# Attention: p times v in two passes over v's two parts, sums of p on VectorE, remainders of p on GpSimd

## The chip, the cores and the metric

One core of a Trainium2 chip runs the whole program in one launch. The metric is the device time of that launch in microseconds, the median of several runs. Five engines work side by side, each through a list of instructions of its own: TensorE (PE, with its weight loads as PEld), VectorE (DVE), ScalarE (ACT), GpSimd (POOL) and SyncE (SP), which here issues most of the transfers. They meet through semaphores alone.

## The reference, cut to what matters

Two requests, of 1024 (prompt) and 2048 (sample) tokens, pass through one layer: RMSNorm, a projection, two groups of attention heads side by side (8 GQA heads over 2 key heads of width 64, and 8 MLA heads of width 96), an output projection, a mixture of experts and a last norm. Both requests see 16 learned meta tokens ahead of their own keys. For each head and each request:

```python
s = jnp.einsum('bqhgd,bkhd->bhgqk', q, k, preferred_element_type=jnp.float32) * scale
p = jax.nn.softmax(s, axis=-1).astype(v.dtype)
return jnp.einsum('bhgqk,bkhe->bqhge', p, v)
```

Everything is float32. The change touches how `p` times `v` and the sums of `p` are computed.

## The kernel before, in words

The program has six stages after each other. The first, `stage_project`, makes q, k and v for all heads and stores them; the second, `stage_attend`, is attention; the four behind it are not touched.

TensorE multiplies in fp32r, which keeps fewer bits than float32. To keep the accuracy, a float32 matrix is written as a high part (rounded to fp32r) and a low part (the remainder, rounded too), and products are added up in several passes.

**Steps of a head.** `ITEMS` lists the work of a head. The queries are taken 512 at a time (six blocks: four of the sample request, two of the prompt). Within a block an item is one group of 128 keys, and one item at the end holds the 16 meta keys; so a sample block has 17 items, a prompt block 9, a head 86. "Step j" is what each engine does around item j:

- TensorE, `qk` (L1071): scores of 128 keys by 512 queries into one of two banks `psS`, two passes in a GQA head, three in an MLA head.
- ScalarE, `exp` (L940, L943): the exponential twice, once rounded as `p_hi`, once in full as `prob`. A meta item has a third one (L942).
- VectorE, `remainder` (L988): `p_lo = prob - p_hi`. Every eighth item from 24 on is done by GpSimd instead (L929), 8 a head. Slots for p are four.
- TensorE, `pv` (L1094), two steps behind: three passes into `psO` with v's part as weights, 64 columns and a column of ones, whose product is the denominator: v_hi with p_hi, v_lo with p_hi, v_hi with p_lo.

**Maxima for the next head.** The exponentials need a maximum for each query beforehand. So during head h, TensorE also makes a rough score of head h+1 (L1102, one pass, 128 queries by 512 keys, bank `psM`, two of them), and VectorE takes its maximum (L996). These are the 80 `UNITS`, spread over 72 of the 86 steps. The meta keys have 24 small products of 16 columns of their own (L1108), all at one step. At step 79 the maxima are turned (`row`, L1115), written to DRAM and read back as one row of q of head h+1 (L863, L866); TensorE waits for it before the next head's first scores.

**End of a block.** ScalarE copies `psO` out (L949), TensorE turns it in four pieces of 65 (L1121), VectorE takes the reciprocal of the denominator and multiplies (`normalise`, L1019, L1022), and the result is stored.

**Loads.** SyncE loads q, k, v of head h+2 in two parts: the sample part once item 67 of head h is through `pv`, then comes the row store of head h+1, then the prompt part at the end of the head. GpSimd splits the loaded v into v_hi and v_lo (`split`, L905, L916).

**The order** is written out by hand: each engine's function walks the same items, and numbers such as `j - 2` for `pv` or `j - 6` for `normalise` say how far behind it works. The heads lie in two loops of two heads a turn, with the last pairs of each kind written out.

In `stage_project` the copy of GQA's v is GpSimd's (L334), MLA's v comes out of a bank `psX` by ScalarE (L416); the two banks of `psX` serve "v", "k", "n", "r", "s" units in turn, and TensorE waits for the bank to be free (L651 for the "k" units).

## Time and profile before

| what | us |
|---|---|
| median of 3 runs | 4235.22 (4228.05 to 4240.24) |
| profiled execution | 4237.25 |
| its span, first to last instruction | 4235.1 |
| TensorE busy in the span | 3738.5 |
| VectorE busy | 2819.2 |
| ScalarE busy | 2366.1 |
| GpSimd busy | 429.1 |
| stage_project, about | 0 to 560 |
| stage_attend, about | 560 to 2875 |

The span counts from the first to the last instruction of the profiled execution; the time of that execution is 2.15 us longer. Busy time is the union of the listed durations on one engine. On TensorE a listed duration includes the way through the array, so that consecutive matmuls overlap in the list. "Released by" names what a waiting instruction waited for, as inferred from semaphores. A duration "x2" in the order in time is the merged length of two instructions in a row.

### The profile page before, as it was taken

Reading aid. Unit: us, or ns where it says so; the run is one execution under the profiler, and the core shown is the slowest. Engines: PE = TensorE matmul, PEld = TensorE weight load, DVE = VectorE, ACT = ScalarE, POOL = GpSimd, SP = SyncE. Lnnn points to the kernel's source line nnn. Section 1 sums busy time; section 2 is a strip of 40 time slices with the busy share of each in tenths; the row PEclk is TensorE's granted clock in tenths of the full one; section 3 lists DMA queues with packets and bytes.
Section 4 is the critical chain, followed back from the end, with each engine's and each line's share of the span. In section 5 each row is a group of like instructions: output and inputs, shape, how many; then the busy total and the mean of one; then the engine's idle time right before and its main releaser. Section 6 shows DMA issues by size and latency. Waiting matters only on the chain. (4 is left out here: it accounts for less than half of the span.)

```text
span 4235.1 us, 60176 instructions
## 1 busy us (share of the span) xinstructions
PE 3738.5 (88%) x16747; PEld 2738.7 (65%) x16748; DVE 2819.2 (67%) x4468; ACT 2366.1 (56%) x4059; POOL 429.1 (10%) x497
## 2 busy tenths in 40 slices
PE   7999856999999999999999999996999499999920
PEld 7989724666666666666666766765777366666610
DVE  5656545888878888777776877743443666666645
ACT  4434303777777777776676766784332155555522
POOL 0000010111111111111011011000000011110123
PEclk9999957999999999999999999998999699999965
DMA  4555574221222211221122022003333277777768
GB/s 161 167 194 194 166 166 160 60 46 26 54 60 60 59 40 28 60 59 42 24 59 60 16 48 60 6 7 141 137 125 113 84 254 249 248 248 248 248 211 295
DMA packets 330198, 495.54 MB, mean 117 GB/s; under 512 B 118791, under 2 KB 261411, under 8 KB 318915
## 3 DMA queue, kind: packets, MB, share of 16 engines
q1 hardware_dynamic: 241798, 359.85, 28.8%
q10 hardware_dynamic: 71888, 73.54, 5.0%
q0 software_dynamic: 16272, 59.25, 4.1%
q8 instruction: 115, 1.88, 0.2%
q14 instruction: 125, 1.02, 0.1%
HBM read 330.84 MB, written 161.78 MB: 116 GB/s over the span
## 5 line engine op out<-in xcount | busy, mean ns | idle before, releaser
L940 ACT ACTIVATE b_p_hi<-b_psS 128x512 fp32r<-128x512 f32 (+1 forms) x1376 | 822.1, 597 | 620.2 <-PE b_psS L1071 579.5
L1071 PE MATMUL b_psS<-b_q,b_k 96*128 96x512 f32 (+3 forms) x3440 | 1053.2, 404 | 53.5 <-ACT b_prob L943 31.6
L988 DVE TENSOR_TENSOR b_p_lo<-b_prob,b_p_hi 128x512 fp32r<-128x512 f32 x1152 | 830.1, 722 | 287.5 <-ACT b_prob L943 248.5
L943 ACT ACTIVATE b_prob<-b_psS 128x512 f32<-128x512 f32 (+1 forms) x1376 | 815.1, 592 | 1.1
L1071 PEld LDWEIGHTS b_psS<-b_q,b_k 96*128 96x128 f32 (+3 forms) x3440 | 629.8, 186 | 285.0 <-ACT b_prob L943 39.2
L996 DVE TENSOR_REDUCE b_mx_s<-b_psM 128x1 f32<-128x512 f32 x1024 | 690.8, 687 | 86.8 <-PE b_psM L1102 66.1
L1102 PE MATMUL b_psM<-b_k,b_q 128*128 128x512 f32 (+1 forms) x1280 | 515.8, 424 | 54.5 <-DMA b_v<-V 39.2
L1094 PE MATMUL b_psO<-b_p_hi,b_v_hi 128*65 128x512 f32 x1280 | 516.9, 404 | 25.8 <-DVE b_p_lo L988 23.9
L1094 PE MATMUL b_psO<-b_p_hi,b_v_lo 128*65 128x512 f32 x1280 | 509.7, 398 | 0.0
L1094 PE MATMUL b_psO<-b_p_lo,b_v_hi 128*65 128x512 f32 x1280 | 509.6, 398 | 0.0
L1102 PEld LDWEIGHTS b_psM<-b_k,b_q 128*128 128x128 f32 (+1 forms) x1280 | 251.8, 197 | 158.2 <-DVE b_mx_s L996 53.1
L929 POOL TENSOR_TENSOR b_p_lo<-b_prob,b_p_hi 128x512 fp32r<-128x512 f32 x128 | 166.7, 1302 | 1720.0 <-ACT b_prob L943 1720.0
L1094 PEld LDWEIGHTS b_psO<-b_p_lo,b_v_hi 128*65 128x65 f32 x1280 | 175.8, 137 | 125.5 <-issue 5.7
L1094 PEld LDWEIGHTS b_psO<-b_p_hi,b_v_hi 128*65 128x65 f32 x1280 | 176.7, 138 | 118.8 <-DVE b_p_lo L988 52.1
L1094 PEld LDWEIGHTS b_psO<-b_p_hi,b_v_lo 128*65 128x65 f32 x1280 | 177.6, 139 | 110.1 <-issue 4.3
L2016 PE MATMUL e_psG<-e_w_gu,e_xT 128*128 x512 | 232.1, 596 | 9.0 <-SPq L1863 8.0
L612 PE MATMUL a_psZ<-a_w_hi,a_xT_hi 128*128 128x396 f32 x600 | 209.2, 349 | 24.2 <-DVE a_w_lo L569 24.2
L1965 DVE TENSOR_TENSOR e_wd_lo<-e_w_dn,e_wd_hi 128x2048 fp32r<-128x2048 f32 x64 | 146.7, 2293 | 104.0 <-ACT e_wd_hi L1914 104.0
L612 PE MATMUL a_psZ<-a_w_hi,a_xT_lo 128*128 128x396 f32 x600 | 206.9, 345 | 0.0
L612 PE MATMUL a_psZ<-a_w_lo,a_xT_hi 128*128 128x396 f32 x600 | 206.3, 344 | 0.0
L996 DVE TENSOR_REDUCE b_mx_p<-b_psM 128x1 f32<-128x512 f32 x256 | 173.9, 687 | 30.8 <-PE b_psM L1102 27.6
L1900 ACT ACTIVATE e_wg_hi<-e_w_gu 128x2048 fp32r x64 | 122.9, 1920 | 98.1 <-SPq L1863 74.7
(246 smaller groups left out, 5184.9 us busy)
## 6 DMA issues: line engine op xcount, KB each, us to landing
e_w_gu<-w_gate SPq DMA_DIRECT2D x32, 1024.0 KB
e_w_gu<-w_up SPq DMA_DIRECT2D x32, 1024.0 KB
e_w_dn<-w_down SPq DMA_DIRECT2D x32, 1024.0 KB
Y<-e_y ACTq DMA_DIRECT2D x64, 512.0 KB, 5.3
Y<-b_zeros ACTq DMA_DIRECT2D x4, 4096.0 KB, 27.3
a_x_raw<-xallT SPq DMA_DIRECT2D x25, 512.0 KB, 5.0
a_x<-xall SPq DMA_DIRECT2D x25, 512.0 KB, 4.4
c_o<-O SPq DMA_DIRECT2D x24, 512.0 KB, 4.9
```

Source lines behind the costliest of these rows:

```text
L612: i = nc.tensor.matmul(psZ[:, b, 0:ZW], xx[:, s, c, :], ww[:, c, b * ZW:b * ZW + ZW], start=n == 0, stop=n == 3 * KC - 1)
L929: nc.gpsimd.tensor_tensor(p_lo[:, slot, :], prob[0:kn, slot, :], p_hi[0:kn, slot, :].bitcast(F32), ALU.subtract).then_inc(lo_ready_pool, 1)
L940: nc.scalar.activation(p_hi[0:kn, (s * NI + j) % NP, :], psS[0:kn, j % 2, :], ACT.Exp)
L943: nc.scalar.activation(prob[0:kn, (s * NI + j) % NP, :], psS[0:kn, j % 2, :], ACT.Exp).then_inc(p_ready, 1)
L988: nc.vector.tensor_tensor(out, prob[0:kn, slot, :], p_hi[0:kn, slot, :].bitcast(F32), ALU.subtract).then_inc(lo_ready, 1)
L996: nc.vector.tensor_reduce(dst, psM[:, u % 2, :], AX.X, ALU.max).then_inc(m_free, 1)
L1071: m = nc.tensor.matmul(psS[0:kn, j % 2, :], kk[s][0:r, k], qq[s][0:r, q], start=n == 0, stop=n == len(passes) - 1)
L1094: m = nc.tensor.matmul(psO[0:VC, b % 2, :], vv[s][:, vc, :], pp[:, slot, :], start=first and n == 0, stop=last and n == 2)
L1102: nc.tensor.matmul(psM[:, u % 2, :], q0[s][0:r, q * P:q * P + P], k0[s][0:r, kc:kc + 512], start=True, stop=True).then_inc(m_psum, 1)
L1900: nc.scalar.activation(wg_hi[:, :, :], w_gu[:, bass.ds(w * KC, HK), :], ACT.Copy).then_inc(wg_rounded, 1)
L1965: nc.vector.tensor_tensor(wd_lo[:, c, :], w_dn[:, bass.ds(w * HC, HC), :], wd_hi[:, c, :].bitcast(F32), ALU.subtract).then_inc(wd_ready, 1)
L2016: nc.tensor.matmul(psG[:, s, :], xT[:, c - HK, :], w_gu[:, bass.ds(w * KC + c, 1), :].rearrange("p o n -> p (o n)"), start=c == HK, stop=F ...
```

## The change

- v is kept as its two parts side by side: 128 columns, high and low, made once in `stage_project` (GpSimd subtracts for GQA, VectorE for MLA) and loaded as such. The column of ones goes. `pv` has two passes, v with p_hi (`pv_hi`, two steps behind) and v with p_lo (`pv_lo`, four steps behind); rows 0 to 63 of the result belong to v's high part and 64 to 127 to its low part, and are added in `normalise`. So p_lo times v's low part is now in the sum as well.
- The denominators: VectorE adds every `prob` of a block into a PSUM bank `acc` (`den_add`), the last sum goes to `accS`; TensorE turns it, VectorE sums along the keys.
- All remainders of 128-key items go to GpSimd; a meta item's stays on VectorE. p has six slots, not four, and a slot is free when both `pv_lo` and the sum are done.
- The meta item is second in a block. The meta keys are stored beside the prompt's and beside the sample's keys, so the maxima see them too: 104 units of 346 to 414 keys over 68 steps, and the 24 small products go. The loads get 3 or 4 more transfers of 16 columns per part.
- `row` is at step 77, the turn of the results at 6 steps behind a block's end (was 5) and with eight transposes of 128x128, `normalise` at 7 (was 6).

```diff
-VC = VD + 1
+VC = 2 * VD
...
+        BY_ACT, BY_DVE = "vkn", "vknrs"
...
+                src = z[:, s, ZV:ZCQ].rearrange("p (h c) -> p h c", c=VD)
                 for copy in range(2):
-                    i = nc.gpsimd.tensor_copy(vst_g[:, b, j, copy:PAIRS:2, 0:VD],
-                                              z[:, s, ZV:ZCQ].rearrange("p (h c) -> p h c", c=VD))
+                    nc.gpsimd.tensor_copy(vst_g[:, b, j, copy:PAIRS:2, 0:VD].bitcast(F32R), src)
+                pool.drain()
+                for copy in range(2):
+                    i = nc.gpsimd.tensor_tensor(vst_g[:, b, j, copy:PAIRS:2, VD:VC].bitcast(F32R), src,
+                                                vst_g[:, b, j, copy:PAIRS:2, 0:VD], ALU.subtract)
                 i.then_inc(v_copied, 1)
...
+                    if kind == "v":
+                        r = META if B is None else P
+                        i = nc.vector.tensor_tensor(vst_m[0:r, j, :, VD:VC].bitcast(F32R),
+                                                    psX[0:r, u % 2, :].rearrange("p (h c) -> p h c", c=VD),
+                                                    vst_m[0:r, j, :, 0:VD], ALU.subtract)
+                    elif kind == "k":
...
+        CUT_S, CUT_P = [414, 414, 412, 412, 412], [348, 346, 346]
+        assert sum(CUT_S) == META + DEC_SEQ and sum(CUT_P) == META + SEQ
...
-        for base, n in ((SEQ, DEC_SEQ), (0, SEQ)):
+        for base, n, k_at, meta_at in ((SEQ, DEC_SEQ, SAMPLE, META_S), (0, SEQ, 0, META_P)):
             for qc in range(base, base + n, W):
-                ch = [(META + base + c * P, P, (base + c * P) // P) for c in range(n // P)] + [(0, META, TILES)]
+                ch = [(k_at + c * P, P, (base + c * P) // P) for c in range(n // P)]
+                ch.insert(1, (meta_at, META, TILES))
...
+        UNITS = []
+        for first, tiles, at, cuts in ((SEQ // P, DEC_SEQ // P, META_S, CUT_S), (0, SEQ // P, 0, CUT_P)):
+            for i in range(tiles):
+                UNITS += [(first + i, at + sum(cuts[:u]), cuts[u], u) for u in range(len(cuts))]
         NU = len(UNITS)
-        R = 4
-        SPAN = 72
+        R = 6
+        HI_LAG, LO_LAG = 2, 4
+        SPAN = 68
...
+                    q, k, sm = slice(SEQ, TOK), (slice(META_S, SAMPLE), slice(SAMPLE, KT)), ld_s[s]
+                    kd = (slice(0, META), slice(META + SEQ, KEYS))
...
+                    for c, d in zip(k, kd):
+                        dma(k0[s][0:GD, c], t["KGH"][rk, d])
+                        dma(k0[s][GD:P, c], t["KGH"][rk, d])
+                        dma(k1[s][0:GD + 1, c], t["KGL"].rearrange("g r n -> (g r) n")[bass.ds(i * (GD + 1), GD + 1), d])
...
+            def remainder(h, s, j):
+
+                if ITEMS[j][2] == META:
+                    return
+                slot = slot_of(s, j)
+                pool.wait_ge(p_ready, h * NI + j + 3)
+                nc.gpsimd.tensor_tensor(p_lo[:, slot, :], prob[:, slot, :], p_hi[:, slot, :].bitcast(F32),
+                                        ALU.subtract).then_inc(lo_ready, 1)
...
+                act.wait_ge(pv_done, h * NI + j + 1 + NP - reuse(s, j))
+                act.wait_ge(den_done, h * NI + j + 1 + NP - reuse(s, j))
+                slot = slot_of(s, j)
+                nc.scalar.activation(p_hi[0:kn, slot, :], psS[0:kn, j % 2, :], ACT.Exp)
+                nc.scalar.activation(prob[0:kn, slot, :], psS[0:kn, j % 2, :], ACT.Exp).then_inc(p_ready, 1)
...
+            def den_add(h, s, j):
+
+                _, _, kn, _, first, last = ITEMS[j]
+                slot = slot_of(s, j)
                 dve.wait_ge(p_ready, h * NI + j + 3)
-                out = p_hi[M_HI2, slot, :] if kn == META else p_lo[:, slot, :]
-                nc.vector.tensor_tensor(out, prob[0:kn, slot, :], p_hi[0:kn, slot, :].bitcast(F32),
-                                        ALU.subtract).then_inc(lo_ready, 1)
+                if kn == META:
+                    nc.vector.tensor_tensor(p_hi[M_LO, slot, :], prob[0:kn, slot, :], p_hi[0:kn, slot, :].bitcast(F32),
+                                            ALU.subtract).then_inc(meta_lo_ready, 1)
+                dve.wait_ge(den_done, h * NI + j + NP)
+                if first:
+                    m = nc.vector.tensor_copy(acc[:, :], prob[:, slot, :])
+                else:
+                    out = accS[:, BLOCK_OF[j] % 2, :] if last else acc[0:kn, :]
+                    m = nc.vector.tensor_tensor(out, acc[0:kn, :], prob[0:kn, slot, :], ALU.add)
+                m.then_inc(den_done, 1)
...
-                tv = psT[:, 0:SUP * VC].rearrange("p (j c) -> p j c", c=VC)
-                nc.vector.reciprocal(rden[:, :].unsqueeze(2), tv[:, :, VD:VC])
+                tv = psO[:, b % 2, :].rearrange("p (j c) -> p j c", c=P)
+                nc.vector.tensor_reduce(den[:, :], psT[:, :].rearrange("p (j c) -> p j c", c=P), AX.X, ALU.add)
                 dve.drain()
+                nc.vector.reciprocal(rden[:, :], den[:, :])
+                dve.drain().then_inc(t_free, 1)
                 dve.wait_ge(o_stored[b % 2], 16 * (h * (NB // 2) + b // 2 + 1))
-                nc.vector.tensor_tensor(ost[:, b % 2, :, :], tv[:, :, 0:VD],
-                                        rden[:, :].unsqueeze(2).broadcast_to([P, SUP, VD]), ALU.mult).then_inc(o_ready, 1)
-                dve.drain().then_inc(t_free, 1)
+                rr = rden[:, :].unsqueeze(2).broadcast_to([P, SUP, VD])
+                nc.vector.tensor_tensor(o_lo[:, :, :], tv[:, :, VD:2 * VD], rr, ALU.mult)
+                nc.vector.tensor_tensor(ost[:, b % 2, :, :], tv[:, :, 0:VD], rr, ALU.mult)
+                dve.drain()
+                nc.vector.tensor_tensor(ost[:, b % 2, :, :], ost[:, b % 2, :, :], o_lo[:, :, :], ALU.add).then_inc(o_ready, 1)
...
+            def pv_hi(h, s, j):
+                _, _, kn, vc, first, _ = ITEMS[j]
+                b = BLOCK_OF[j]
+                if kn == META:
+                    return
+                pe.wait_ge(p_ready, h * NI + j + 3)
                 if first:
...
+                    cc = slice(c * P, c * P + P)
+                    nc.tensor.transpose(psO[:, b % 2, cc], oT[:, b % 2, cc], ident[:, :])
+                    m = nc.tensor.transpose(psT[:, cc], accS[:, b % 2, cc], ident[:, :])
...
-                    pv(h, s, j - 2, block_of[j - 2])
-                    if j - 5 in END_OF:
-                        o_turn(h, END_OF[j - 5], use(h, END_OF[j - 5], last))
+                    pv_hi(h, s, j - HI_LAG)
+                    pv_lo(h, s, j - LO_LAG)
+                    if j - 6 in END_OF:
+                        o_turn(h, END_OF[j - 6], use(h, END_OF[j - 6], last))
...```

Two places in the order of instructions, with what each waits for. VectorE, GQA heads, where a block's normalise stands between two steps; `b_psM` is the bank of maxima, `b_psT` the bank the results are turned into. Before:

```order
L988 TENSOR_TENSOR b_p_lo<-b_prob,b_p_hi 128x512 [waits b_p_ready]
L994 REGISTER_ALU
L996 TENSOR_REDUCE b_mx_s<-b_psM 128x1 [waits b_m_psum]
L1017 REGISTER_ALU
L1019 RECIPROCAL b_rden<-b_psT 128x4 [waits b_t_psum]
L1022 TENSOR_TENSOR b_ost<-b_psT,b_rden 128x256 [waits b_o_stored1]
L986 REGISTER_ALU
L988 TENSOR_TENSOR b_p_lo<-b_prob,b_p_hi 128x512 [waits b_p_ready]
```

After the change:

```order
L1000 TENSOR_TENSOR b_acc<-b_acc,b_prob 128x512 [waits b_den_done]
L1006 REGISTER_ALU
L1008 TENSOR_REDUCE b_mx_s<-b_psM 128x1 [waits b_m_psum]
L1006 REGISTER_ALU
L1008 TENSOR_REDUCE b_mx_s<-b_psM 128x1 [waits b_m_psum]
L1025 REGISTER_ALU
L1027 TENSOR_REDUCE b_den<-b_psT 128x4 [waits b_t_psum]
L1029 RECIPROCAL b_rden<-b_den 128x4
L1033 TENSOR_TENSOR b_o_lo<-b_psO,b_rden 128x256 [waits b_o_stored1]
L1034 TENSOR_TENSOR b_ost<-b_psO,b_rden 128x256
L1036 TENSOR_TENSOR b_ost<-b_ost,b_o_lo 128x256
L995 REGISTER_ALU [waits b_p_ready]
```

A sum takes the place of each remainder, some steps have two maxima, and normalise has five instructions for two. TensorE, GQA heads, around one step. Before:

```order
L1071 MATMUL b_psS<-b_q_0,b_k_0 128x512 [waits b_p_ready]
L1071 MATMUL b_psS<-b_q_0,b_k_0 128x512
L1102 MATMUL b_psM<-b_k_1,b_q_1 128x512 [waits b_m_free] x2
L1094 MATMUL b_psO<-b_p_hi,b_v_hi 65x512 [waits b_lo_ready_pool]
L1094 MATMUL b_psO<-b_p_hi,b_v_lo 65x512
L1094 MATMUL b_psO<-b_p_lo,b_v_hi 65x512
```

After the change:

```order
L1115 MATMUL b_psM<-b_k_1,b_q_1 128x412 [waits b_m_free] x2
L1096 MATMUL b_psO<-b_p_hi,b_v 128x512 [waits b_p_ready]
L1108 MATMUL b_psO<-b_p_lo,b_v 128x512 [waits b_lo_ready]
L1084 MATMUL b_psS<-b_q_0,b_k_0 128x512 [waits b_p_ready]
L1084 MATMUL b_psS<-b_q_0,b_k_0 128x512
```

The third pass is gone, the products with v are 128 wide, and the two of a step are of different items with a wait of their own.

## Rows read from the trace of the kernel before

**Rows 1.** Windows: us, then PE, PEld, DVE, ACT, POOL busy (x), clock, DMA, GB/s.

```profile
1300.00:1700.00 400.00, 392.51 (x1744) 265.71 (x1742) 344.47 (x561) 314.16 (x588) 55.91 (x47) 1.00 0.23 50
```

**Rows 2.** The order in time, one GQA step: start us, us, engine, line, operation.

```profile
1007.39 0.64 PE L1071 MATMUL b_psS<-b_q,b_k 128*128 128x512 f32 x2
...
1008.79 0.62 PE L1071 MATMUL b_psS<-b_q,b_k 128*128 128x512 f32 x2
...
1007.71 0.68 DVE L996 TENSOR_REDUCE b_mx_s<-b_psM 128x1 f32<-128x512 f32 x1
...
1008.31 0.68 DVE L988 TENSOR_TENSOR b_p_lo<-b_prob,b_p_hi 128x512 fp32r<-128x512 f32 x1
```

**Rows 3.** The order in time: meta-key products; then row stores; last, the stores' own line.

```profile
1421.27 0.39 PE L1090 MATMUL b_psO<-b_p_hi,b_v_meta 128*65 128x512 f32 x1
...
1445.49 0.39 PE L1090 MATMUL b_psO<-b_p_hi,b_v_meta 128*65 128x512 f32 x1
...
2400.32 0.40 PE L1090 MATMUL b_psO<-b_p_hi,b_v_meta 128*65 128x512 f32 x1
...
2428.27 0.40 PE L1090 MATMUL b_psO<-b_p_hi,b_v_meta 128*65 128x512 f32 x1
...
811.49 0.31 SPq L863 DMA_DIRECT2D MX<-b_nmxT  x1
...
1714.34 0.30 SPq L863 DMA_DIRECT2D MX<-b_nmxT  x1
...
L863 SPq DMA_DIRECT2D MX<-b_nmxT x16: 302/308/1948, 655.8 to 2737.4; - x16
```

**Rows 4.** The order in time, first stage: nine transposes of 128x128.

```profile
410.93 1.14 PE L623 MATMUL a_psR<-a_ident,a_stage 128*128 128x128 f32 x9
```

**Rows 5.** The order in time, VectorE: one block's normalise and what follows.

```profile
942.59 0.18 DVE L1019 RECIPROCAL b_rden<-b_psT 128x4 f32<-128x4 f32 x1 [0.17 <-issue]
...
942.93 0.42 DVE L1022 TENSOR_TENSOR b_ost<-b_psT,b_rden 128x256 f32<-128x256 f32 x1 [0.16 <-issue]
...
943.56 0.69 DVE L988 TENSOR_TENSOR b_p_lo<-b_prob,b_p_hi 128x512 fp32r<-128x512 f32 x1 [0.21 <-issue]
```

**Rows 6.** The page's part 5: remainders on GpSimd; busy, mean ns, idle before.

```profile
L929 POOL TENSOR_TENSOR b_p_lo<-b_prob,b_p_hi 128x512 fp32r<-128x512 f32 x128 | 166.7, 1302 | 1720.0 <-ACT b_prob L943 1720.0
```

**Rows 7.** The order in time beside GpSimd's split; then line 1022's min/median/max ns.

```profile
943.75 2.78 POOL L916 TENSOR_TENSOR b_v_lo<-b_v,b_v_hi 128x1040 fp32r<-128x1040 f32 x1
...
944.44 2.65 DVE L988 TENSOR_TENSOR b_p_lo<-b_prob,b_p_hi 128x512 fp32r<-128x512 f32 x1 [0.18 <-ACT b_prob L943]
...
L1022 DVE TENSOR_TENSOR b_ost<-b_psT,b_rden x96: 423/425/426, 727.9 to 2869.7; 128x256 f32<-128x256 f32 x96
```

**Rows 8.** The order in time, TensorE after three waits; then windows from 1080.

```profile
947.14 0.44 PE L1094 MATMUL b_psO<-b_p_hi,b_v_hi 128*65 128x512 f32 x1 [1.46 <-DVE b_p_lo L988]
...
1080.28 0.69 PE L1094 MATMUL b_psO<-b_p_hi,b_v_hi 128*65 128x512 f32 x1 [2.08 <-DVE b_p_lo L988]
1080.76 0.63 PE L1094 MATMUL b_psO<-b_p_hi,b_v_lo 128*65 128x512 f32 x1
...
957.77 1.22 PE L1071 MATMUL b_psS<-b_q,b_k 128*128 128x512 f32 x2 [4.95 <-issue]
...
1080.00:1085.00 5.00, 4.72 (x14) 2.69 (x15) 1.90 (x4) 2.27 (x5) 0.00 (x0) 0.66 0.05 12
```

**Rows 9.** The order in time, SyncE's issues; then one window while they run.

```profile
1320.03 0.49 SPq L828 DMA_DIRECT2D b_q<-QGH  x1
...
1336.03 1.95 SPq L863 DMA_DIRECT2D MX<-b_nmxT  x1
1340.40 0.23 SPq L866 DMA_DIRECT2D b_q<-MX  x1
...
1325.00:1335.00 10.00, 10.00 (x58) 7.26 (x56) 6.71 (x14) 6.96 (x14) 0.56 (x1) 1.00 1.01 215
```

**Rows 10.** Groups by line, first stage: the product that waits for v's eviction.

```profile
L651 PEld LDWEIGHTS a_psX<-a_ckvT,a_w_kup 128*128 128x128 f32 x104 | 18.8, 194 | 28.5 <-ACT a_vst_m L416 25.2 <-issue 1.3
```

243 lines of the change are left out of this document (95 added, 148 removed).

## The prediction

> **What bounds the kernel now.** I read the page first, then stretches of the attention stage, then single instructions there. The page puts TensorE first and VectorE second over the whole span. Attention alone is tighter: in 400 us of it TensorE is busy 392.5, VectorE 344.5, ScalarE 314.2 and GpSimd 55.9, at full clock [rows 1]. TensorE sets the pace there, with VectorE 14% behind.
>
> Busy time counts the whole length of an instruction, though the next one starts earlier, so I price by start to start. A 512-column matmul is listed as 0.39 us, but the next starts after 0.23: the six of a GQA step run from 1007.39 to 1008.79, so 0.232 each (1.40 a step), with 65 or with 128 columns of weights. On VectorE, remainder and maximum alternate at exactly 0.60, though listed as 0.68 [rows 2]. These two prices carry most of the sum.
>
> The spacing of one meta-key product to the next gives the time of a block. A sample block of 17 steps takes 24.2 us in a GQA head, 28.0 in an MLA head. The last head has no maxima to make; its blocks come to 23.2 by the prices (100 matmuls). The row of maxima is written once a head: 7 GQA heads take 1714.34-811.49, 129.0 each, and 7 MLA heads 2737.4-1714.34, 146.2 each [rows 3]. A check of the prices: a GQA head now has 498 full-width matmuls, 115.5 us, plus some 9 of narrow ones, transposes and stalls, against 126 to 134 measured.
>
> **The change on TensorE.** The third pass goes: 80 matmuls x 0.232 = 18.6 us a head. The 24 meta maxima of 16 columns go as well. Units become 104 instead of 80; at 412 columns one should take 0.19 us (0.232 less 100 columns at 2.4 GHz), so +1 us. The 24 narrow transposes become 48 of 128x128; nine such took 1.14 us [rows 4], so 6 us a head. A GQA sample block then needs 67x0.232 + 26x0.19 + 1.0 = 21.5 us, an MLA block 17 passes more, 25.4.
>
> **The change on VectorE.** The length of an instruction grows by 1.02 ns an element (128x256 is 0.42, 128x512 is 0.68 [rows 2, 5]), so a 412-column maximum costs 0.60-0.10 = 0.50. Per sample block:
> - 16 sums at 0.60 = 9.6. They replace 14 remainders; GpSimd had two.
> - The meta item has two dependent instructions, 2x0.69, and one of them reads two SBUF tensors and can wait for GpSimd, 0.5 on average: 1.9.
> - 26 maxima at 0.50 (now 19 at 0.60) = 12.9.
> - Normalise. Now: drain, reciprocal, drain, multiply, 1.14 us from the end of the work before to the next start [rows 5]. It gets a 512-element sum (0.69), a second multiply (0.34), an add (0.43) and two more gaps of 0.16, and the add can wait 0.5 for GpSimd: 3.3.
>
> Together 27.7 us, **more than TensorE needs in either kind of head**; by the same prices it is 22.2 now. For a whole head: 3 such blocks, plus 35 steps with two short blocks (32 sums 19.2, 3 meta items 5.7, 3 normalises 9.9, 26 maxima 12.3, row work 1.5 = 48.6): 131.7 us.
>
> No row shows a sum that reads and writes PSUM. From above it is bounded by the isolated 0.69, from below by 0.53 (512 elements at that slope); I take 0.60, since the maximum, which reads PSUM, and the remainder, which reads SBUF, keep the same pace in the same stretch [rows 2]. The ends are -6 and +8 us a head. The Trainium skill (VectorE: DVE Perf Modes, the section on the TRN2 errata) charges a PSUM source 120 cycles where an SBUF source pays 58. By that the estimate would be 65 ns more for each sum, some 5.5 us a head and about 85 us on the kernel. By that rule a maximum out of PSUM would last longer than a remainder out of SBUF; the trace has both at 0.68.
>
> **GpSimd** takes all 80 remainders of a head at 1.30 (1.32 with a gap) [rows 6], 104 us, and loses the splitting of v. Of the 27.7 of a block it needs 20.8, so VectorE covers it. Where the units end (18 steps) it needs about 21 against VectorE's 22. Only in the last head does it set the pace: 16 at 1.32 and 0.5 for the meta item, 21.6 a block against 23.2; with the short blocks 8 us in all.
>
> **Contention.** GpSimd's split already holds VectorE up: at 944.44 a remainder lasts 2.65 us beside a subtraction of 2.78 on GpSimd, while the multiply of PSUM with SBUF never varied, 423 to 426 ns over 96 [rows 7]. So I charge the port only where VectorE reads two SBUF tensors, and to the sums nothing. The Trainium skill (SBUF — State Buffer, "Who interferes with whom") states just this, that a second SBUF input contends and a single one does not; were the sums held all the same, see rival 2.
>
> **What lies between the sums.** VectorE will not be busy without a gap. Normalise comes in one lump of 3.3 us and TensorE can run only two maxima ahead, so it stalls some 2 to 3 us a block. After a stall of 1.46 it went on at full pace; after one of 2.08 its matmuls came 0.48 apart, and the slow spell of 3.5 us after it costs 1.7; the granted clock of that stretch, 0.66, mixes the 1.2 and the 2.4 GHz level [rows 8]. In a GQA head VectorE's backlog hides most of that; I charge 0.5 a block, 28.2. In an MLA head TensorE has 25.4 to do, and stall 2.0 plus clock 1.4 give 28.8.
>
> The row of maxima gets tight. The sample loads of the head after next (3.7 MB at 215 GB/s, 17 us and a start) begin at 1320.03 and so drain about 1338; the row store issued at 1336.03 lets its reload start only at 1340.40 [rows 9]. v's two halves make it 4.2 MB, 19.5 us, and the loads start two steps later (remainder pass four steps behind). That is 15 steps before the boundary, some 20 us, while drain, store and reload need 24. The other end is that v's 260-byte pieces, doubled, cost nothing: then 1.5 us are missing. I charge 2 us of idle VectorE a head, and 2 for the pause of 4.95 us at a loop's turn, which stays [rows 8]; 2 more in MLA heads. That makes GQA 3x28.2+48.6+3.8 = **137**, MLA 3x28.8+48.6+6 = **141**.
>
> **The first stage.** TensorE already waits for the eviction of v (25.2 us in total before the next product, over 12 batches) [rows 10]. Two subtractions of 0.69 now follow it before the bank is free: +0.75 a batch, 9 us. Its GpSimd subtractions lie behind matmuls. Larger first loads and more units before the first head: +3. Later stages are untouched.
>
> **Sum.** 8 GQA heads x (+8) = +64; 7 MLA heads x (-5.2) = -36; last head -8; +9; +3: +32. The profiled execution was 4237.25 around a span of 4235.1, 2 above the median of 4235.22, so against the median 4267.
>
> **Rivals.**
> 1. *The lumps are absorbed.* If VectorE really never waits (six slots of p instead of four let it lag), heads cost 131.7 of either kind: +2.7x8 -14.5x7 -8+12 = -76, so 4159, faster. For: all other engines then have slack. Against: maxima have two banks only, and waits for them occur already. It decides if the stall at normalise stays under 1.5 us. Chance 0.27.
> 2. *GpSimd's port holds the sums too.* Then 80 pairs cost 1.30+0.60 in turn, 152 a head before the other work: some +20 a head, 4560. [rows 7] speak against it. 0.05.
> 3. *Sums or stalls cost more.* Each sum takes the isolated 0.69 (+8 a head), or each lump ends at the 1.2 GHz level and the row waits 4 to 5 us (+4 to +7): 4330 to 4390. The page on VectorE's modes (the Trainium skill, above) gives much the same for the sums. 0.16.
> 4. *No gain from the narrower array use*: a 128-column v load could slow a pass; [rows 2] show 128-column passes at the same pace. With 0.03 more for each of 166 passes MLA heads would cost 5 more, 4300. 0.02.
>
> My own account, ending +0.3 to +2%, gets 0.34. Between it and rival 1 lies a balance within 0.3% (12.7 us, about what a measurement of this kernel can tell from no change), 0.14, and a small gain, 0.02. Slower: 0.34+0.05+0.16+0.02 = 0.57; faster: 0.27+0.02 = 0.29; same 0.14. The low end is rival 1 at 4150; the high end 4370 holds rival 3 and the PSUM price, and leaves out rival 2.
>
> **What would show it.** Right: VectorE over 93% busy in the stretches of attention, sums 0.60 apart, maxima of 412 at 0.50, TensorE idle before maxima for VectorE, sample blocks of 28 us in both kinds of head, stalls over 2 us before the maximum behind each normalise. Wrong: MLA blocks at 26 or less; sums over 0.9 long beside GpSimd; GpSimd named as what TensorE waits for inside sample blocks; the first stage more than 20 us later.

## The result and the profile after

The changed kernel takes 4393.81 us (median of 4 runs, 4388.29 to 4415.98), the kernel before 4237.73 (4 runs, 4228.05 to 4249.32): ratio 1.0377, 95% interval 1.0332 to 1.0422. It is slower, as forecast, but by 3.8% and not 0.8%: the forecast of 4267 was 127 us too low, and the top of the range, 4370, was too low as well. The profiled execution took 4394.57 us around a span of 4392.6; the differences below are between the two spans, 157.5 us.

First the windows of the attention stage after the change, GQA and then MLA heads, in the columns of [rows 1].

```profile
1300.00:1700.00 400.00, 348.24 (x1388) 247.47 (x1389) 351.38 (x651) 265.54 (x496) 285.65 (x224) 0.93 0.18 43
2100.00:2500.00 400.00, 358.32 (x1497) 276.04 (x1497) 322.48 (x590) 249.41 (x464) 267.02 (x209) 0.93 0.23 54
```

TensorE had 392.5 of 400 us [rows 1] and now has 348.2, VectorE has 351.4: no engine is full. The forecast wanted VectorE over 93%; it is 88% busy, and in MLA heads 81%. The granted clock is 0.93, which mixes the 1.2 and 2.4 GHz levels; before the change it was 1.00 in the first of these stretches and 0.97 in the second.

The pitch is the time from one block's meta-key product to the next. Here are these products of two GQA blocks and two MLA blocks, in the order in time on TensorE; then the stores of the row on SyncE (line, count, ns min/median/max).

```profile
1472.16 0.49 PE L1103 MATMUL b_psO<-b_p_hi,b_v_meta 48*128 48x512 f32 x1
...
1501.08 0.49 PE L1103 MATMUL b_psO<-b_p_hi,b_v_meta 48*128 48x512 f32 x1
...
2086.49 0.49 PE L1103 MATMUL b_psO<-b_p_hi,b_v_meta 48*128 48x512 f32 x1
...
2117.17 0.49 PE L1103 MATMUL b_psO<-b_p_hi,b_v_meta 48*128 48x512 f32 x1
...
L889 SPq DMA_DIRECT2D MX<-b_nmxT x16: 303/7586/9322, 678.1 to 2918.8; - x16
```

This GQA block takes 28.9 us (24.2 in [rows 3], the shortest of that head's sample blocks; the two ahead of it take 24.6 and 24.7), this MLA block 30.7 (28.0). The row's store, 308 ns in the median before, takes 7.6 us. What TensorE waits for over the whole attention stage (us in total, times, longest) shows two places, the maxima and the row; the third row is the prologue.

```profile
PE b_psM L1115 <- DVE b_mx_s L1008: 128.7, 151, 2.6
PE b_psS L1084 <- DMA b_q<-MX: 76.9, 15, 7.4
...
PE b_psM L1115 <- DMA b_v<-V: 44.8, 1, 44.8
```

With the prompt's maxima the waits for `b_psM` come to 173.7 us in 200 waits. Of these 55 are longer than 2 us, three or four a head; each ends 1.1 to 1.2 us after a normalise's addition. In the kernel before, the wait for the reloaded row was a single one of 3.6 us, at the first head.

By the reloads of the row, as [rows 3] count by stores, the 157.5 us lie here:

| part | before | after | difference of all | forecast |
|---|---|---|---|---|
| up to the reload of the first row | 657.2 | 679.4 | +22.2 | +12 |
| first head | 156.6 | 172.4 | +15.8 | +8 |
| next 7 GQA heads, each | 129.0 | 144.1 | +106 | +56 |
| 7 MLA heads, each | 146.0 | 151.3 | +37 | -36 |
| last head | 130.8 | 119.1 | -12 | -8 |
| later stages | 1365.7 | 1353.3 | -12 | 0 |

The change does not touch the last line. In the twelve profiles of the experiments the later stages take 1369 to 1380 us, also where the attention stage is the changed one, so the 1353.3 of this profile is scatter and no gain. It matters below: a difference between this profile and another one has some 15 to 27 us of these stages in it, and the attention stage is compared by heads and blocks.

VectorE's lump of work at a block's end, in the order in time: one normalise, then the two instructions of TensorE around the stall that it makes in a GQA head, and the same in an MLA head with the window behind it.

```profile
1504.55 0.69 DVE L1027 TENSOR_REDUCE b_den<-b_psT 128x4 f32<-128x512 f32 x1 [0.17 <-issue]
...
1505.61 0.42 DVE L1033 TENSOR_TENSOR b_o_lo<-b_psO,b_rden 128x256 f32<-128x256 f32 x1
1505.95 0.42 DVE L1034 TENSOR_TENSOR b_ost<-b_psO,b_rden 128x256 f32<-128x256 f32 x1
1506.44 0.69 DVE L1036 TENSOR_TENSOR b_ost<-b_ost,b_o_lo 128x256 f32<-128x256 f32 x1
1507.05 0.69 DVE L1000 TENSOR_TENSOR b_acc<-b_acc,b_prob 128x512 f32<-128x512 f32 x1
```

```profile
1505.20 0.62 PE L1084 MATMUL b_psS<-b_q,b_k 128*128 128x512 f32 x2
1508.28 0.46 PE L1115 MATMUL b_psM<-b_k,b_q 128*128 128x414 f32 x1 [2.46 <-DVE b_mx_s L1008]
...
2094.14 0.57 PE L1115 MATMUL b_psM<-b_k,b_q 96*128 96x414 f32 x1 [2.34 <-DVE b_mx_s L1008]
2094.51 0.63 PE L1096 MATMUL b_psO<-b_p_hi,b_v 128*128 128x512 f32 x1
2094.94 0.63 PE L1108 MATMUL b_psO<-b_p_lo,b_v 128*128 128x512 f32 x1
```

```profile
2093.50:2097.00 3.50, 2.85 (x8) 2.33 (x9) 2.79 (x6) 0.12 (x1) 0.77 (x1) 0.62 0.18 37
```

Stalls over 2 us behind normalise are there, 2.46 and 2.34, and so is a slow spell behind them: passes 0.43 apart in place of 0.235, a clock of 0.62 over 3.5 us. Not every stall has one: at 44 of the 55 the granted clock falls to the 1.2 GHz level during the stall or within 3 us of its end, at 11 it doesn't. That gives the price of the spell. Two GQA blocks, then two MLA blocks, each from meta product to meta product, without a spell and with one:

```profile
1180.60:1208.23 27.63, 24.30 (x102) 16.89 (x101) 26.39 (x50) 18.93 (x36) 20.37 (x17) 1.00 0.03 6
1472.16:1501.08 28.92, 25.56 (x102) 18.35 (x101) 26.61 (x50) 18.94 (x36) 20.39 (x17) 0.94 0.03 6
2057.20:2086.49 29.29, 26.62 (x120) 20.86 (x119) 26.90 (x50) 18.91 (x36) 20.53 (x17) 1.00 0.02 6
2086.49:2117.17 30.68, 28.15 (x119) 22.21 (x118) 27.14 (x50) 18.92 (x36) 20.56 (x17) 0.94 0.02 5
```

A spell costs 1.3 us in a GQA block and 1.4 in an MLA block. Without one a GQA block takes 27.6, which is VectorE's sum of 27.7, with TensorE's stall inside it.

The prices, by line (count, ns min/median/max), then GpSimd's remainders as the page's part 5 has them:

```profile
L1000 DVE TENSOR_TENSOR b_acc<-b_acc,b_prob x1184: 678/689/700, 686.9 to 3035.3; 128x512 f32<-128x512 f32 x180, 16x512 f32<-16x512 f32 x18
...
L1036 DVE TENSOR_TENSOR b_ost<-b_ost,b_o_lo x96: 425/772/1540, 753.0 to 3041.2; 128x256 f32<-128x256 f32 x96
...
L993 DVE TENSOR_TENSOR b_p_hi<-b_prob,b_p_hi x96: 680/681/1880, 686.0 to 3026.1; 16x512 fp32r<-16x512 f32 x96
```

```profile
L929 POOL TENSOR_TENSOR b_p_lo<-b_prob,b_p_hi 128x512 fp32r<-128x512 f32 x1280 | 1640.2, 1292 | 880.5 <-ACT b_prob L949 865.8
```

The sum over PSUM lasts 0.69 as the remainder did [rows 5], and its 1184 instances lie between 678 and 700 ns, beside a GpSimd that is busy 286 of 400 us. Only the two operations with two SBUF inputs stretch (to 1540 and 1880 ns).

### The profile page after: what moved, and what is told of

Read it like the earlier page. It is cut to its first block and busy times, and to the rows that moved or that the text cites. A ratio compares the mean times of both kernels' runs of the same rounds, so it can differ in the third digit from the quotient of the medians.

```text
span 4392.6 us, 62310 instructions
## 1 busy us (share of the span) xinstructions
PE 3684.1 (84%) x15851; PEld 2809.0 (64%) x15852; DVE 3098.6 (71%) x5356; ACT 2307.5 (53%) x3963; POOL 1820.5 (41%) x1586
## 5 line engine op out<-in xcount | busy, mean ns | idle before, releaser
L929 POOL TENSOR_TENSOR b_p_lo<-b_prob,b_p_hi 128x512 fp32r<-128x512 f32 x1280 | 1640.2, 1292 | 880.5 <-ACT b_prob L949 865.8
L1084 PE MATMUL b_psS<-b_q,b_k 96*128 96x512 f32 (+3 forms) x3440 | 1104.1, 420 | 124.7 <-DMA b_q<-MX 76.9
L1000 DVE TENSOR_TENSOR b_acc<-b_acc,b_prob 128x512 f32<-128x512 f32 (+1 forms) x1184 | 818.9, 692 | 131.6 <-ACT b_prob L949 109.8
L1084 PEld LDWEIGHTS b_psS<-b_q,b_k 96*128 96x128 f32 (+3 forms) x3440 | 651.3, 195 | 323.1 <-issue 87.6
L949 ACT ACTIVATE b_prob<-b_psS 128x512 f32<-128x512 f32 (+1 forms) x1376 | 817.2, 594 | 0.0
L1115 PE MATMUL b_psM<-b_k,b_q 128*128 128x412 f32 (+7 forms) x1664 | 608.9, 408 | 220.3 <-DVE b_mx_s L1008 128.7
L1008 DVE TENSOR_REDUCE b_mx_s<-b_psM 128x1 f32<-128x412 f32 (+1 forms) x1280 | 702.7, 579 | 107.6 <-PE b_psM L1115 105.4
L1115 PEld LDWEIGHTS b_psM<-b_k,b_q 128*128 128x128 f32 (+1 forms) x1664 | 339.8, 204 | 479.8 <-DVE b_mx_s L1008 283.2
L1096 PE MATMUL b_psO<-b_p_hi,b_v 128*128 128x512 f32 x1280 | 537.1, 420 | 0.3 <-ACT b_prob L949 0.3
L1108 PE MATMUL b_psO<-b_p_lo,b_v 128*128 128x512 f32 x1280 | 533.5, 417 | 0.7 <-POOL b_p_lo L929 0.7
L1096 PEld LDWEIGHTS b_psO<-b_p_hi,b_v 128*128 128x128 f32 x1280 | 259.6, 203 | 34.2 <-issue 4.0
L1108 PEld LDWEIGHTS b_psO<-b_p_lo,b_v 128*128 128x128 f32 x1280 | 260.6, 204 | 18.2 <-POOL b_p_lo L929 1.0
L1008 DVE TENSOR_REDUCE b_mx_p<-b_psM 128x1 f32<-128x346 f32 (+1 forms) x384 | 184.7, 509 | 15.3 <-PE b_psM L1115 14.6
```

Of the source, the lines that this page charges most:

```text
L929: nc.gpsimd.tensor_tensor(p_lo[:, slot, :], prob[:, slot, :], p_hi[:, slot, :].bitcast(F32), ALU.subtract).then_inc(lo_ready, 1)
L949: nc.scalar.activation(prob[0:kn, slot, :], psS[0:kn, j % 2, :], ACT.Exp).then_inc(p_ready, 1)
L1000: m = nc.vector.tensor_tensor(out, acc[0:kn, :], prob[0:kn, slot, :], ALU.add)
L1008: nc.vector.tensor_reduce(dst, psM[:, u % 2, 0:n_keys], AX.X, ALU.max).then_inc(m_free, 1)
L1084: m = nc.tensor.matmul(psS[0:kn, j % 2, :], kk[s][0:r, k], qq[s][0:r, q], start=n == 0, stop=n == len(passes) - 1)
L1096: nc.tensor.matmul(psO[:, b % 2, :], v[s][:, vc, :], p_hi[:, slot_of(s, j), :], start=first, stop=False)
```

## The experiments

Two questions. *Do the stall and the clock behind normalise lie on top of the heads' work (A), or is VectorE's sum of work what sets the time, so that it hides them (B)?* And: *what makes the row late, and is its wait on the path (C), or does the same time only move (D)?* Twelve kernels ran. The kernel before took 4241.91 to 4245.10 us in the median beside them; ratios are to it, with their 95% intervals.

**e1: ScalarE stores and reloads the row itself.** Edit: the row leaves SyncE, whose queue is behind the loads.

```
-                row(h + 1, 1 - s, nxt)                     # SyncE
+                    if not last and j == STORE_AT:         # ScalarE, ROW_AT + 2
+                        act.wait_ge(row_made, h + 2)
+                        act.dma_start(t["MX"]..., nmxT[:, :].bitcast(F32)).then_inc(row_kept, 16)
```

> ScalarE instead of SyncE stores the row of maxima (at step 79) and reads it back (step 81), so that it no longer stands behind the sample loads in SyncE's queue. No work is removed. Theory A (stalls of TensorE at the row and at normalise, and the slow clock behind each, lie on top of VectorE's work): the waits for the row, 5.4 to 7.4 us in GQA heads and 3.3 to 4.8 in MLA heads, fall to nearly nothing; with the clock behind them 5 to 7 us a head, 4290 to 4320. Theory B (VectorE's own work, 131.7 us a head, sets the time and hides the wait in its backlog): less than 15 us, 4380 to 4395.

Measured: 4424.34 us, ratio 1.0412 (1.0359 to 1.0464). That is outside both forecasts; it isn't faster than the change, and the intervals of the two overlap, so it isn't clearly slower either. In the list of waits, ScalarE's and TensorE's:

```profile
ACT b_oT L955 <- DMA MX<-b_nmxT: 85.3, 14, 7.2
...
PE b_psO L1136 <- ACT b_oT L955: 90.6, 20, 7.6
```

The issue of the 12 KB store takes ScalarE 0.3 us, but from there to the reload it still takes 7.4 to 9.8 us in the 14 heads with loads, and now a busy engine waits for it. So it isn't its place in SyncE's queue alone that holds it; the 4 MB of loads are under way all the same, and e9 takes them away from in front of it.

**e2: normalise in three pieces** (denominators at step 7, multiplies at 8, addition at 9).

```
-                    if j - 7 in END_OF: normalise(...)
+                    if j - 7 in END_OF: norm_den(...)
+                    if j - 8 in END_OF: norm_mul(...)
+                    if j - 9 in END_OF: norm_add(...)
```

> Normalise in three pieces at steps 7, 8 and 9 behind a block's end (sum and reciprocal; the two multiplies; the add) instead of all at step 7. No work is removed or added. Theory A: no stall of TensorE over 1.5 us before a maximum, granted clock in sample blocks back to about 1.0, blocks 27.7 to 28 us in GQA heads (now 28.9) and 28 to 28.6 in MLA heads (now 30.7); 4280 to 4320. Theory B: VectorE has as much to do as before, so blocks stay within 0.3 us and the time within 15 us of 4394.

Measured: 4365.98, ratio 1.0299 (1.0255 to 1.0343), 28 us better than the change: between A (4280 to 4320) and B (within 15 us of 4394). The same work without its lump: GQA blocks 27.9 (28.9), MLA blocks 29.0 (30.7), clock 0.97 in both windows of 400 us. Heads take 142.1 (144.1) and 146.3 (151.3). So some of A is there, 1.0 and 1.7 a block, with the work unchanged. But the changed kernel's own blocks without a slow spell take 27.6 and 29.3: what spreading gains is the clock, and of the stall itself next to nothing.

**e3: normalise takes v's high half alone.** It leaves the low half's product out of the result: one multiply, one gap and the addition less.

```
-                nc.vector.tensor_tensor(o_lo[:, :, :], tv[:, :, VD:2 * VD], rr, ALU.mult)
...
-                nc.vector.tensor_tensor(ost[...], ost[...], o_lo[:, :, :], ALU.add)
```

> The low half of the result is left out: normalise has no second multiply, no add and no gap between them (some 1.3 us less a block), so the output lacks the product with v's low part. Theory A: the stall falls from 2.4 to about 1.1 us, which is short enough to keep the clock, so a GQA block gains 1.3 to 2 us and an MLA block 3 to 4: 4170 to 4230. Theory B: just VectorE's 1.3 us, 90 blocks, in both kinds of head: 4275 or so.

Measured: 4276.65, ratio 1.0069 (1.0037 to 1.0102). That is B's 4275, but not by B's way, 1.3 us in every block. GQA blocks take 26.5 and MLA blocks 27.9, which is 2.4 and 2.8 shorter than the blocks with a slow spell and 1.1 and 1.4 shorter than those without. So in a GQA block VectorE's work comes back, in an MLA block the shorter stall (1.0 to 1.1 in place of 2.34), and in both the clock: no stall over 1.5 us is left, and in MLA heads no spell inside the three middle blocks. GQA heads gain 7.6 us, MLA heads 10.9.

**e4: of the sums only a block's first and last.** The denominators are incomplete, and VectorE loses some 14 sums of 0.60 a block.

```
+                if not first and not last:
+                    dve.sem_inc(den_done, 1)
+                    return
```

> Of the sums of p only the first and the last of a block are made (14 of 16, and the meta item's, left out), so the denominators are wrong; everything else stays. VectorE loses about 9 of 27.7 us a sample block. If VectorE is what bounds both kinds of head, GQA blocks fall from 28.9 to 22 or 23 us (TensorE 21.5, GpSimd 21) and MLA blocks from 30.7 to 26 or 27 (TensorE 25.4); 4030 to 4120. If GpSimd's remainders or the slots of p are what binds, GQA blocks stay above 25.

Measured: 4284.65, ratio 1.0102 (1.0047 to 1.0156), far above the 4030 to 4120 expected. The windows of the two stretches:

```profile
1300.00:1700.00 400.00, 354.58 (x1477) 265.43 (x1476) 252.37 (x466) 284.09 (x536) 306.02 (x241) 0.94 0.24 55
2100.00:2500.00 400.00, 368.77 (x1612) 293.43 (x1610) 237.48 (x440) 265.52 (x495) 284.23 (x222) 0.96 0.20 44
```

Over 8 us of a block's work leave VectorE, which now idles some 40%, and blocks still take 24.8 to 26.7 (GQA) and 27.8 to 29.4 (MLA): the lower value of each without a slow spell, the upper one with one. All 55 stalls are left, at 1.7 to 2.0 us. B alone cannot be: VectorE has time to spare, and the block stays long. Nor is it GpSimd or the slots of p, for which TensorE hardly waits here; it waits for the maxima and the row. Of the 24.8 TensorE waits 1.8, so its own part is 23.0 and not the 21.5 of the forecast. e3 and e4 together say that a block without a spell is about the longer of two sums, VectorE's work, and TensorE's work with its stall; a spell adds 1.3 to 1.8 on top.

**e5: only q goes ahead of the row.** SyncE issues q of the head after next, then the row, then k and v.

```
-                    load(h + 2, i + 1, s, kind, "s")
+                    load(h + 2, i + 1, s, kind, "s", kv=False)
                 row(h + 1, 1 - s, nxt)
+                if more:
+                    load(h + 2, i + 1, s, kind, "s", kv=True)
```

> The changed kernel with one move on SyncE's queue: of the sample loads of the head after next only those of q go ahead of the row of maxima (store and reload), those of k and v follow behind the row. Theory C (the wait for the row at the head's boundary is time on the path, and it is the megabytes in front of the small store that make it): the 5.4 to 7.4 us (GQA) and 3.3 to 4.8 us (MLA) waits of TensorE for the reloaded row fall under 1 us, GQA heads come to about 137 us, MLA heads to about 147, the kernel to 4290 to 4320 us. Rival D (the same transfers are only late elsewhere): the k and v loads now land some 5 us later than before, and TensorE waits for them before the first maximum of the next head instead; the kernel stays within 15 us of 4394. Rival B (VectorE's sum of work sets the heads): VectorE catches up during the wait at the boundary, so that without it the blocks get longer and the kernel stays above 4360.

Measured: 4344.98, ratio 1.0246 (1.0205 to 1.0286), between C and D and below the 4360 of B. The store of the row is back at 0.3 us and its wait is gone, but before the next head's first maximum TensorE shows a new one:

```profile
1421.59 0.71 PE L1123 MATMUL b_psM<-b_k,b_q 128*128 128x414 f32 x1 [4.58 <-DMA b_v<-V]
```

Heads take 139.4 and 148.4: some 3 to 5 us a head came back, and as much turned into the wait for k and v (10 times, 3.1 to 6.0 us, beside the 44.6 of the prologue).

**e6b: e5, and normalise taken apart with its addition on GpSimd.**

```
+            def add(h, b):                                  # GpSimd, two steps behind the denominators
+                pool.wait_ge(mul_done, h * NB + b + 1)
+                nc.gpsimd.tensor_tensor(ost[...], ost[...], o_lo[:, :, :], ALU.add).then_inc(o_ready, 1)
```

> The changed kernel with the order of e5 and with normalise taken apart: VectorE does the sum of the denominators and the reciprocal behind step 7 of the block, its two multiplies one step later, and the addition of the two halves goes to GpSimd (80 remainders and 5 additions a head). Results are stored three steps later. Theory A (the stall behind each normalise and the clock it costs lie on top of the work): VectorE's work per sample block falls from 27.7 to about 26.7 us, no stall over 1.9 us is left, the clock is 0.97 or more, GQA blocks take 25.5 to 26.7 us and MLA blocks 27 to 28, GQA heads about 128 and MLA heads about 134, the kernel 4120 to 4180 us. Rival B (VectorE's sum of work alone sets the pace): only the 1.0 us a block that leave VectorE come back, 5 a head, so 75 us in all on top of what e5 gives, about 4230 if e5 gives 4305. Rival E (GpSimd's addition, in turn with remainders of 1.3 us each, and its port hold the next block up): a wait for GpSimd shows before the first v pass of a block, and the kernel stays above 4300.

Measured: 4308.94, ratio 1.0174 (1.0142 to 1.0206); A expected 4120 to 4180 and missed, and E's total, above 4300, is met. Of the stalls before maxima two over 1.5 us are left, but with the shorter ones they still sum to 128.5 us (173.7 in the changed kernel). GQA blocks are 27.2 and MLA blocks 28.6, but TensorE now waits for VectorE's meta remainder, 2.8 to 3.1 us at six of the boundaries and 3.7 to 4.0 in the last head, whose sample blocks go from 20.9 to between 26.2 and 27.0. The last head alone takes 27 us more than in e5, which hides much of what the MLA heads gain (141.6 for 148.4). The order in time on GpSimd and VectorE at one boundary, VectorE's in the last head, and that line over the whole run:

```profile
1406.10 0.73 POOL L945 TENSOR_TENSOR b_ost<-b_ost,b_o_lo 128x256 f32<-128x256 f32 x1
1406.78 6.25 POOL L938 TENSOR_TENSOR b_p_lo<-b_prob,b_p_hi 128x512 fp32r<-128x512 f32 x5
...
1407.35 6.22 DVE L1020 TENSOR_TENSOR b_p_hi<-b_prob,b_p_hi 16x512 fp32r<-16x512 f32 x1
...
2827.74 8.07 DVE L1020 TENSOR_TENSOR b_p_hi<-b_prob,b_p_hi 16x512 fp32r<-16x512 f32 x1 [0.53 <-ACT b_prob L972]
...
L1020 DVE TENSOR_TENSOR b_p_hi<-b_prob,b_p_hi x96: 680/682/8067, 685.7 to 2926.5; 16x512 fp32r<-16x512 f32 x96
```

An addition puts GpSimd behind, so that its next five remainders run without a gap, and a 0.68 us operation of VectorE with two SBUF inputs lasts 6.22 us, until that run is over. Rival E named the port, though as a wait for GpSimd; what the rows show is VectorE shut out for a whole run.

**e7: no low part of v for the MLA heads.** VectorE's subtraction in the first stage is left out, that half is zero.

```
-        BY_ACT, BY_DVE = "vkn", "vknrs"
+        BY_ACT, BY_DVE = "vkn", "knrs"
```

> The changed kernel without the low part of the MLA heads' v: VectorE's 0.69 us subtractions in the first stage are left out and that part is held at zero, so the bank of the v products is free sooner (the output lacks what the low part adds for these heads). My term for the first stage: the last product of it comes 9 to 10 us earlier (553.4 goes to about 544), the attention stage stays, the kernel comes to about 4384. Rival F (the first stage is longer for its larger stores of v or for GpSimd's subtractions for the GQA heads): the stage keeps 10 us or more of its extra 13.7 us.

The last group of the first stage on TensorE, of e7 and then of the changed kernel:

```profile
541.37 0.92 PE L663 MATMUL a_psX<-a_cqT,a_w_qup 128*128 128x256 f32 x3 [0.65 <-DVE a_stage L548]
```

```profile
553.43 0.91 PE L662 MATMUL a_psX<-a_cqT,a_w_qup 128*128 128x256 f32 x3 [0.52 <-DVE a_stage L548]
```

The group starts 12.1 us earlier, of the 13.7 by which the change had put it off; my term was 9. The place of the stage's end moves by itself from profile to profile: its last product starts between 556.5 and 561.1 us in the ten profiles with the subtraction and at 548.2 here, so the gain lies between 8 and 13. The waits behind the eviction don't move: 35.7 to 36.1 us in all ten, 25.2 in e7 as in the kernel before. That makes 10.5 for the subtraction. The kernel as a whole takes 4401.29 (2 runs, 4392.24 to 4410.34; ratio 1.0394, 1.0345 to 1.0443), where 4384 was expected. In its profile the attention stage is 7 us longer than in that of the changed kernel and the later stages, which the edit doesn't touch, 21 us longer; two runs don't settle a difference of 12.

**e8: the meta keys beside the key groups, alone,** on the kernel before; three passes, remainders and denominators stay.

```
-        UNITS = [(SEQ // P + i, META + SEQ + u * 512, u) for i in range(DEC_SEQ // P) for u in range(4)]
-        UNITS += [(i, META + u * 512, u) for i in range(SEQ // P) for u in range(2)]
+        CUT_S, CUT_P = [414, 414, 412, 412, 412], [348, 346, 346]
+        for first, tiles, at, cuts in ((SEQ // P, DEC_SEQ // P, META_S, CUT_S), (0, SEQ // P, 0, CUT_P)):
+            for i in range(tiles):
+                UNITS += [(first + i, at + sum(cuts[:u]), cuts[u], u) for u in range(len(cuts))]
```

> One part of the change alone, on the kernel before: the meta keys stand beside the key groups, so the maxima are taken in 104 groups of 412 to 414 and 346 to 348 keys, and the 24 small meta products, their maximum and the last minimum go. Passes of p times v, denominators and remainders stay as before. Theory A: TensorE loses the 24 small products (about 5 us a head by the gap between the last maximum of 512 and the next step) and gains 24 wider ones less 100 columns each (+1); VectorE's sample block goes from 22.2 to about 23.8 us, still under TensorE's 24.2: 15 heads x (1 to 4) us faster, the kernel at 4175 to 4225. Rival G (26 maxima in a block in place of 19 are 26 waits for two banks, and VectorE at 23.8 of 24.2 has no slack for its normalise): stalls before maxima appear, the clock falls below 0.96, and the kernel takes 4240 or more.

Measured: 4222.56 (10 runs), ratio 0.9951 (0.9929 to 0.9974): a small gain, at the slow end of A's range. GQA heads 128.7 (129.0 before), MLA 141.9 (146.0). Sample blocks grow (GQA 24.7 to 25.4, or 24.2 to 24.8 for the one of [rows 3]), since seven more maxima come in each, and the blocks of the prompt shrink by what the 24 products took.

**e9: q and k are loaded when the last score product is done, v behind the row** with a semaphore of its own.

```
-                    sp.wait_ge(pv_done, h * NI + SAMPLE_LAST + 1 + NP)
+                    sp.wait_ge(s_psum, h * NI + SAMPLE_LAST + 1)
                     load(h + 2, i + 1, s, kind, "s")        # q and k
                 row(h + 1, 1 - s, nxt)
+                    sp.wait_ge(pv_done, h * NI + SAMPLE_LAST + 1 + NP)
+                    load_v(h + 2, i + 1, s, kind, "s")
```

> The changed kernel; on SyncE the loads of q and k for the head after next start when the last score product of their buffer is done (four steps earlier than after the last v pass), and v has a semaphore of its own and is loaded behind the row; maxima wait only for q and k. Theory C (the row waits for the megabytes issued in front of it, and what remained in the run with q alone in front was the wait of the first maximum for v's load): both waits go, the boundary costs under 1 us besides the loop's pause, GQA heads come to 137 to 138 us, MLA heads to about 147, the kernel to 4290 to 4315. Rival D (the head needs all its transfers in the time it has, whatever the order): a DMA wait of 3 us or more a head stays somewhere, and the kernel stays above 4335.

Measured: 4311.91, ratio 1.0148 (1.0107 to 1.0190): C, inside its range. SyncE's issues around the row in the changed kernel, then in e9:

```profile
1412.73 0.50 SPq L853 DMA_DIRECT2D b_q<-QGH  x1
...
1422.07 7.38 SPq L889 DMA_DIRECT2D MX<-b_nmxT  x1
1433.49 0.22 SPq L892 DMA_DIRECT2D b_q<-MX  x1
```

```profile
1372.74 0.50 SPq L855 DMA_DIRECT2D b_q<-QGH  x1
...
1388.50 0.31 SPq L895 DMA_DIRECT2D MX<-b_nmxT  x1
1390.23 0.23 SPq L898 DMA_DIRECT2D b_q<-MX  x1
1392.25 0.41 SPq L883 DMA_DIRECT2D b_v<-V  x1
```

From the row's store to its reload it takes 11.4 us in the changed kernel and 1.7 in e9. TensorE's waits for the row are gone but for the first, 3.6 us. Heads come to 137.4 (144.1) and 146.0 (151.3): the row was worth 6.7 and 5.3 a head, with 9.9 in the first head 94 us by the two profiles. The medians differ by 82, since the later stages of the changed kernel's profile are the short ones.

**e10: TensorE adds the halves and the denominators.** The output block is turned by products with two stacked identities, the sums by products with a column of ones; VectorE is back to a reciprocal and a multiply.

```
-                    nc.tensor.transpose(psO[:, b % 2, cc], oT[:, b % 2, cc], ident[:, :])
-                    m = nc.tensor.transpose(psT[:, cc], accS[:, b % 2, cc], ident[:, :])
+                    nc.tensor.matmul(psT[:, at:at + VD], oT[:, b % 2, cc], fold[:, :], start=True, stop=True)
+                    m = nc.tensor.matmul(psT[:, at + VD:at + VD + 1], accS[:, b % 2, cc], ones[:, :], start=True, stop=True)
```

> The changed kernel with normalise made short on VectorE: TensorE turns the output block by products with two identities on top of each other (128x64), which adds the two halves of v, and makes the denominators by products of the sums with a column of ones. The 8 transposes of a block become 8 products of 64 and 1 columns, and VectorE has one reciprocal and one multiply again, as before the change. Theory A (the lump at normalise makes stall and clock loss): VectorE's sample block falls from 27.7 to about 25.6 us, the stalls behind normalise go, the clock is 0.97 or more, GQA blocks take 25.6 to 26.0, MLA blocks 26.0 to 26.7, five blocks a head. GQA heads about 131 and MLA heads about 134 with the row's wait still there (6 and 4 us), the kernel 4140 to 4200. Rival B (VectorE's sum of work alone): GQA the same, but MLA blocks that were 30.7 fall only by the 2.1 us that leave VectorE, to 28.6: 4230 to 4260. Rival H (a product of plain float32 costs more than its columns say): TensorE shows over 0.3 us for each of the 4 products of 64 columns, and blocks stay at 27 or more.

Measured: 4312.54, ratio 1.0142 (1.0095 to 1.0189), above A (4140 to 4200) and B (4230 to 4260). No stall over 1.1 us is left before a maximum. GQA blocks 27.0, MLA 28.4, most of them without a slow spell. Of the changed kernel and of e11, which has the same products, the order in time on TensorE from the meta product on:

```profile
1501.51 0.33 PE L1129 MATMUL b_psO<-b_ident,b_oT 128*128 128x128 f32 x1
1501.67 0.27 PE L1130 MATMUL b_psT<-b_ident,b_accS 128*128 128x128 f32 x1
...
1502.35 0.72 PE L1084 MATMUL b_psS<-b_q,b_k 128*128 128x512 f32 x2
```

```profile
1431.42 0.43 PE L1142 MATMUL b_psT<-b_fold,b_oT 128*128 128x64 f32 x2
1431.69 0.33 PE L1143 MATMUL b_psT<-b_ones,b_accS 128*128 128x1 f32 x2
...
1433.23 0.72 PE L1096 MATMUL b_psS<-b_q,b_k 128*128 128x512 f32 x2
```

Eight transposes take 0.84 us, the four pairs of products 1.81: each plain float32 product is recorded as two, one with 64 columns costs 0.25 and one with a single column 0.20. H wanted over 0.3 for the first, so its price is not met, but its sign, blocks of 27 or more, is. The last head, where no maxima are made, shows the cost: its sample blocks go from 20.9 to between 21.8 and 23.4, and it takes 8.5 us more. 2.1 us of VectorE's work are gone, and a GQA block falls by 1.9, an MLA block by 2.3. That looks like B's arithmetic and isn't: against blocks of the changed kernel without a slow spell (27.6 and 29.3) it is 0.6 and 0.9, the rest is the clock. A's 25.6 for VectorE's block was too low by 1.4.

**e11: e9 and e10 together.**

> Both of the last two edits together: short normalise, and q and k loaded four steps earlier with v behind the row. Theory A with C: the gains add, GQA heads about 126 to 128, MLA heads about 130 to 132, the kernel 4060 to 4120 us, faster than the kernel before the change. Rival B with D: above 4200.

Measured: 4245.49 (10 runs), ratio 0.9998 (0.9982 to 1.0014): 148 us of the loss are undone, and the kernel is level with the one before. Heads 131.7 and 141.4, where before had 129.0 and 146.0. The expected 4060 to 4120 missed, with GQA blocks that would not go under 27.0; the other forecast, above 4200, is met.

**e12: e8, and the stores that clear Y on SyncE.**

```
-                act.dma_start(t["Y"]...)                    # ScalarE, after the fourth exponential
+                sp.dma_start(t["Y"]...)                     # SyncE, after the first row
```

> The kernel before with the meta keys merged into the key groups (as in the run of that part alone) and one thing that the change does not touch: the four 4 MB stores that clear Y are issued by SyncE behind the first row of maxima, not by ScalarE in the middle of the first head. In every profile of this study ScalarE's fifth exponential starts some 32 us late behind their issue, and TensorE idles 28 to 30 us in front of it. Theory I (the issue itself holds ScalarE, and nothing else needs those 30 us): the gap falls under 2 us, the heads stay at 126 to 134 and 138 to 148 us, and the kernel takes 4190 to 4198 us, faster than the kernel before and than the changed one. Rival J (the stores' 16 MB at 350 GB/s hold up what comes after them, the first head's own result stores and the loads behind them on SyncE): under 15 us come back.

In the order in time, ScalarE in the kernel before, then SyncE in e12:

```profile
666.19 8.62 ACTq L956 DMA_DIRECT2D Y<-b_zeros  x2
...
674.83 24.16 ACTq L956 DMA_DIRECT2D Y<-b_zeros  x2
699.24 0.60 ACT L940 ACTIVATE b_p_hi<-b_psS 128x512 fp32r<-128x512 f32 x1 [31.98 <-issue]
```

```profile
662.48 33.05 SPq L884 DMA_DIRECT2D Y<-b_zeros  x4
```

The issue lasts as long, on an engine with nothing else to do then, and ScalarE's gap of 32 us is gone. Measured: 4188.48, ratio 0.9882 (0.9854 to 0.9909), the fastest of the study and 34 us less than e8; theory I holds, 1.5 us under its range. The first head goes from 161.6 to 128.4.

## Why the prediction was right or wrong

**Right: the direction and what turns it.** VectorE has more to do in a GQA block than TensorE: a block without a slow spell takes 27.6, VectorE's forecast sum is 27.7, and TensorE's own part is 23.0 (e4; forecast 21.5). Blocks of the two kinds of head come close together (28.9 and 30.7), and stalls over 2 us stand behind three or four normalises of a head. Passes saved on TensorE buy nothing in a GQA head. With the row's wait taken out (e9), GQA heads take 137.4 where 137 was forecast, but that is luck: the 137 has 2 us for the row in it, and they stand in for three blocks that were priced 0.7 too low.

**Right: the single prices.** The sum costs what the remainder did. The Trainium skill (VectorE: DVE Perf Modes, the TRN2 errata) would have a PSUM source dearer by 62 cycles; 689 ns against the remainder's 690 [rows 5] don't show it. Sums with one SBUF input are not held by GpSimd, operations with two are, for up to 6.22 and 8.07 us in e6b. The Trainium skill (SBUF — State Buffer, "Who interferes with whom") says that one SBUF input doesn't contend, that two do, and that the shared ports are an exclusive lock; the 1184 sums and the two groups of 96 above agree. Rival 2 is out. Passes with 128 columns of v stay 0.235 apart: rival 4 is out.

**Wrong: "I charge 2 us of idle VectorE a head" for the row.** The arithmetic beside it (15 steps are 20 us, drain, store and reload need 24) pointed to 4, and I took 2, between 4 and next to nothing. Measured: waits of 5.4 to 7.4 us (GQA) and 3.3 to 4.8 (MLA), and by e9 the row was worth 6.7 and 5.3 a head. Against the 2 charged (4 in MLA heads) that is 8x4.7 and 7x1.3, some 47 us of the 127. From its issue to the reload the store took 11 to 13 us, and still 7.4 to 9.8 from another engine's queue (e1). Rival 3 had this mechanism and a price of 4 to 5 for the wait.

**Wrong: the MLA block, 28.8 for 30.7.** By the sum it was 25.4 + 2.0 + 1.4; the terms were the right ones and two were too small. At full clock the block from 2057.2 to 2086.5 takes 29.3, of which TensorE waits 2.7: its work is 26.6, not 25.4. Of that 1.2, passes 0.235 apart and not 0.232 make 0.25, and the meta product, 0.74 from the pass before it to the transposes, some 0.3; the rest I did not find. Where the clock falls behind the stall, 1.4 come on top: 26.6 + 2.7 + 1.4 = 30.7. Three blocks are 5.7 us of MLA's miss of 10 a head and the row 1.3; the rest lies in the stretch with the short blocks, which I priced by VectorE's work alone, with no stall and no spell.

**Wrong: "VectorE's backlog hides most of that", the GQA block, 28.2 for 28.9.** I let the backlog hide stall and slow clock but for 0.5. It hides the stall: a block at full clock takes 27.6. It doesn't hide the clock: with a spell the block takes 28.9, and VectorE's own waits over 0.25 us go from 0.6 to some 1.5 a block, since TensorE is late with the next maximum. Rival 3 in its second form had it so, each lump ending at the 1.2 GHz level and the row waiting 4 to 5 us: 4330 to 4390, the nearest of all. The addition in normalise lasts 0.77 in the median, inside the 0.93 that its price and its wait had in the sum.

**Wrong in size: the first stage and the prologue, 12 for 22.** The subtractions of v cost 10.5 and not 9: the first product behind an eviction now waits 35.7 us in all in place of 25.2 [rows 10], and e7 brings back just that. The first stage is 13.7 longer between these two profiles; the other 3 are less than its end moves by itself. Behind it 8.5 stand against the 3 priced, of which 5.6 are the larger first loads (44.8 us of wait in place of 39.2).

**The miss added up.** By the two spans the miss is 125 us. The row is 47 of it, the GQA blocks 8x3x0.7 = 17, the MLA blocks 7x3x1.9 = 40 and the part up to the first row 10. The last head and the later stages take 16 off, and some 27 are left for the stretches with the short blocks, which no run took apart. These are estimates from the two profiles. The errors share a sign: I took each wait as if the engines had slack to catch up behind it. They have little, in GQA heads by VectorE's sum (27.6 of 28.9) and in MLA heads by TensorE's work (26.6 of 30.7), so a slow spell comes out in full in both, and a wait of TensorE does so in MLA heads.

## To carry to other kernels

Moving work from the fullest engine to the second fullest is worth their difference at most; here that was 14%, and 27.7 against 24.2 in a block used it up before any wait was counted. When two engines are near full, ask of each stall whether the other engine's sum hides it, and count the slow spell behind it in full all the same. Then spread lumps over steps (e2). A small transfer on the path belongs ahead of the large ones: start those earlier, by the semaphore of the last reader and not of the last user of the head (e9), and give what is needed later its own semaphore. And look at the engine that issues a large transfer: four stores of 4 MB held ScalarE for 32 us, which cost the kernel more (34 us, e12) than the change to the maxima brought (19 us, e8).

## What the hardware showed that was not expected

- Four stores of 4 MB occupy the engine that issues them for 33 us, ScalarE (8.62 and 24.16) and SyncE (33.05) alike.
- One operation of VectorE with two SBUF inputs was shut out by five back-to-back GpSimd operations and lasted 6.22 us, and 8.07 us behind the rest of a run of eight (e6b). In the changed kernel, where GpSimd's operations take 1.29 us each, it lasts at most 1.54 for 0.43 and 1.88 for 0.68.
- A 12 KB store that SyncE issues behind 4 MB of loads holds its queue 7.1 to 9.3 us in place of 0.3. From ScalarE's queue the issue takes 0.3 again, but the reload still follows only 7.4 to 9.8 us later (e1), in place of 1.3 to 3.2 with the loads moved (e9).
- A plain float32 product of one column takes 0.20 us, one of 64 columns 0.25, a transpose of 128 columns 0.11 (e11 and the changed kernel): narrow float32 products are no cheap way to add.
- Of the changed kernel's 55 stalls of 2.3 to 2.6 us 44 have a spell at the 1.2 GHz level that begins during them or within 3 us, of e4's 55 of 1.7 to 2.0 us 34, of e2's 101 of 0.5 to 1.5 us 12, and of e10's 66 of 0.5 to 1.1 us none. Spells also come with no such stall right before them: from 1187.5 to 1194.5 of e10 TensorE is busy for all 7.0 us and the granted clock is 0.76. So a stall is not their only cause. Around a stall of 0.64 in e11 this window shows 1.00:

```profile
2229.00:2232.00 3.00, 2.36 (x11) 1.59 (x10) 3.00 (x6) 1.37 (x4) 2.55 (x2) 1.00 0.21 44
```

What stays open: why GQA blocks stop at 27.0 in e10 and e11 where VectorE's prices add up to 25.6 (in the block from 1403.85 to 1431.0 of e11 VectorE waits 1.6 us for one maximum's product, and its meta remainder, two SBUF inputs again, goes up to 1.75 in this kernel; that would be enough for the 1.4, but no run takes either out), and whether the changed form pays if it is used in MLA heads alone, where e11's 141.4 only matches e8's 141.9.
